# First block's value projection computed token by dimension in a two-layer kernel on one Trainium2 core

## The reference, cut to what matters

```
u = rmsnorm(x, g_mix_pre)
proj = u @ w_in                                  # (256, 2048) @ (2048, 10240)
qa, ka, va, qb, kb, vb, gla, glb = split(proj)   # 12 + 12 + 12 heads A, 4 + 4 + 4 heads B of 128, two gates of 2048
ya = dilated_mixture_attention(qa, ka, va) @ w_branch_a    # sum over keys: probs (q, k) @ v (k, 128)
yb = stick_breaking_attention(qb, kb, vb) @ w_branch_b     # likewise w (q, k) @ v (k, 128)
```

## Time and profile before

| what | value |
|---|---|
| median of 3 runs | 2671.86 us (2671.49 to 2672.24) |
| span of the profiled execution | 2672.7 us (first to last instruction; the page gives no other time of it) |
| PE busy | 2642.9 us, 99% of the span, 22834 matmuls |
| DVE busy | 1804.4 us, 68% |
| ACT busy | 1274.7 us, 48% |
| DMA | 496.71 MB, mean 186 GB/s |
| mean granted TensorE clock | 0.995 |

### The profile page before, as it was taken

The page is one execution under the profiler, slowest core; times in us unless marked ns, Lnnn a source line. Parts: engine busy times, 40 slices in busy tenths (PEclk is TensorE's granted clock), DMA queues, the critical chain, the costliest instruction groups (busy, mean ns, idle before and its releaser), DMA issues.

```text
span 2672.7 us, 57540 instructions
## 1 busy us (share of the span) xinstructions
PE 2642.9 (99%) x22834; PEld 2628.9 (98%) x22834; DVE 1804.4 (68%) x2269; ACT 1274.7 (48%) x1548; POOL 249.9 (9%) x206
## 2 busy tenths in 40 slices
PE   9999999999999999999999999999999999999998
PEld 9999999999999999999999999999999999999998
DVE  5455555747888888864467999867576777775444
ACT  5334455345344444444455556554455555554442
POOL 1000000030000000001101665400100000000000
PEclk9999999999999999999999999999999999999999
DMA  7665556574555655556656555556656666666664
GB/s 256 193 199 175 150 161 182 169 213 148 173 195 196 196 194 189 196 191 203 192 168 200 174 163 157 155 183 200 194 183 195 196 194 193 191 190 197 195 191 141
DMA packets 137806, 496.71 MB, mean 186 GB/s; under 512 B 15425, under 2 KB 15425, under 8 KB 137537
## 3 DMA queue, kind: packets, MB, share of 16 engines
q1 hardware_dynamic: 137520, 494.20, 59.7%
q10 hardware_dynamic: 144, 0.52, 0.1%
HBM read 492.57 MB, written 2.10 MB: 185 GB/s over the span
## 4 chain that ended last, share of the span: by engine, by line
PE 89%; DVE 6%; DVEq 2%; ACT 1%; DMA 1%; issue 1%; ACTq 0%; SPq 0%
PE bank L432 86%; DVE w_lo L982 2%; PE ps_a L432 1%; PE ps_o L432 1%; PE ps_n L432 1%; DVE act_lo L1021 1%; PE ps_t L432 0%; DMA hT<-in_xT 0%; ACT w_hi L676 0%; DMA w_raw<-in_w_in 0%; ACT act_hi L742 0%; DVE hT L1046 0%; DVE pr L1309 0%; DVE rstd L1005 0%; DVEq L1299 0%
## 5 line engine op out<-in xcount | busy, mean ns | idle before, releaser
L982 DVE TENSOR_TENSOR w_lo<-w_raw,w_hi 128x1024 fp32r<-128x1024 f32 x928 | 1134.1, 1234 | 720.8 <-ACT w_hi L676 719.2
L676 ACT ACTIVATE w_hi<-w_raw 128x1024 fp32r<-128x1024 f32 x928 | 977.0, 1056 | 1185.9 <-PE bank L432 1045.3
L432 PE MATMUL bank<-act_hi,w_hi 128*128 128x256 f32 x5408 | 1275.3, 279 | 3.0 <-DVE gate_y L1350 2.5
L432 PE MATMUL bank<-act_lo,w_hi 128*128 128x256 f32 x5408 | 1264.9, 277 | 0.0
L432 PEld LDWEIGHTS bank<-act_hi,w_hi 128*128 128x128 f32 x5408 | 1014.9, 188 | 4.1 <-issue 2.7
L432 PEld LDWEIGHTS bank<-act_lo,w_hi 128*128 128x128 f32 x5408 | 1015.7, 188 | 0.7
L432 PE MATMUL bank<-act_hi,w_lo 128*128 128x256 f32 x5408 | 726.9, 277 | 2.7 <-DVE w_lo L982 2.7
L432 PEld LDWEIGHTS bank<-act_hi,w_lo 128*128 128x128 f32 x5408 | 666.6, 188 | 3.1 <-DVE w_lo L982 3.1
L432 PE MATMUL bank<-f_lo,w_hi 128*128 128x256 f32 x1408 | 327.9, 276 | 0.0
L432 PE MATMUL bank<-f_hi,w_hi 128*128 128x256 f32 x1408 | 327.9, 276 | 0.0
L432 PEld LDWEIGHTS bank<-f_lo,w_hi 128*128 128x128 f32 x1408 | 264.3, 188 | 0.0
(11 more groups left out here) (227 smaller groups left out, 1790.3 us busy)
## 6 DMA issues: line engine op xcount, KB each, us to landing
w_raw<-in_w_up SPq DMA_DIRECT2D x352, 512.0 KB, 4.2
w_raw<-in_w_in SPq DMA_DIRECT2D x252, 512.0 KB, 4.2
w_raw<-in_w_down SPq DMA_DIRECT2D x176, 512.0 KB, 4.2
w_raw<-in_w_out SPq DMA_DIRECT2D x64, 512.0 KB, 4.4
w_raw<-in_w_ple_gate SPq DMA_DIRECT2D x32, 512.0 KB, 4.5
w_raw<-in_w_branch_attn SPq DMA_DIRECT2D x16, 512.0 KB, 3.9
w_raw<-in_w_branch_a SPq DMA_DIRECT2D x8, 512.0 KB, 4.1
w_raw<-in_w_branch_b SPq DMA_DIRECT2D x8, 512.0 KB, 3.5
```

The lines of the kernel that those rows point to most:

```text
L432: return pe.matmul(o, l, r, start=start, stop=stop, skip_group_check=True)
L676: act.activation(w_hi[:, k, 0:n, :], w_raw[:, k, 0:n, :], ACT.Copy).then_inc(hi_ready, 1)
L982: dve.tensor_tensor(w_lo[:, k, 0:n, :], w_raw[:, k, 0:n, :], w_hi[:, k, 0:n, :].bitcast(F32), ALU.subtract).then_inc(lo_ready, 1)
```

## The change

A new attribute `by_token` of a stage lists slots that are projected the other way round: a 128x128 tile of the activation (dimensions by tokens) is the stationary operand, and the 256 columns of the weight move. The result has tokens on the partitions and 256 output dimensions along the free side. The number of matmuls of a piece stays 24, and their size stays 128x128 by 256. `st_in` now ends after ka (6 bodies: 2 written out, 4 in the loop); a new stage `st_v` projects va (3 bodies: 1 written out, 2 in the loop), all of its slots by token; in `st_mix` slots 4 and 5 (vb) are by token.

With tokens on the partitions the norm's factor is one number for each partition. PE turns `rstd` once: after piece 15 of `st_in` two fp32 matmuls of one moving column each write the factors of tokens 0 to 127 and 128 to 255 into columns 256 and 257 of `ps_n`, and DVE copies them into `rstd_at` before its first piece of `st_v`. The eviction of a by-token slot is two multiplications of 128x256 by a scalar for each partition. `turn_values`, the 8 copies of ACT and all waits on `v_kept` are gone; two waits move to `pt_kept` and to the eviction count of DVE.

```diff
@@ buffers and semaphores
+        rstd_at = sb("rstd_at", [P, 2])
-        sb("before_stages", [P, 8])
+        sb("before_stages", [P, 6])
-        v_turned, v_kept = sem("v_turned"), sem("v_kept")
+        rstd_ready, rstd_turned = sem("rstd_ready"), sem("rstd_turned")
+        v_turned = sem("v_turned")
@@ stages
-        st_in = Stage("in", pair("w_in"), QB // 4, act_x, main_x(SPLIT["mix"]), "dve")
+        st_in = Stage("in", pair("w_in"), VA // 4, act_x, main_x(SPLIT["mix"]), "dve")
+        st_v = Stage("v", [cols("w_in", 16, 0, 2 * G, VA * P), cols("w_in", 16, 0, 2 * G, (VA + 2) * P)],
+                     HEADS_A // 4, act_x, None, "dve")
+        st_v.by_token, st_mix.by_token = (0, 1), tuple(range((VB - QB) // 2, (GATE_A - QB) // 2))
@@ PE, stream
+                        if s in st.by_token:
+                            for t in range(n):
+                                x = j * PIECE_KT + t
+                                for c in range(2):
+                                    o = ps[:, c * GROUP:(c + 1) * GROUP]
+                                    mm(o, xh[:, x, c * P:(c + 1) * P], w_hi[:, k, t, :], j == 0 and t == 0 and c == 0, False)
+                                    mm(o, xl[:, x, c * P:(c + 1) * P], w_hi[:, k, t, :], False, False)
+                            pe.wait_ge(lo_ready, q + 1)
+                            for t in range(n):
+                                x = j * PIECE_KT + t
+                                for c in range(2):
+                                    last = mm(ps[:, c * GROUP:(c + 1) * GROUP], xh[:, x, c * P:(c + 1) * P], w_lo[:, k, t, :],
+                                              False, j == st.pieces[s] - 1 and t == n - 1)
+                            last.then_inc(piece_used, 1)
+                            ...
+                            continue
@@ PE, beside the pieces
-            def turn_values(n):
-                ...
+            def turn_rstd(piece):
+                if piece == 15:
+                    pe.wait_ge(rstd_ready, 1)
+                    mm(ps_n[:, TOK:TOK + 1], rstd[:, 0:P], ident[:, 0:1], True, True)
+                    mm(ps_n[:, TOK + 1:TOK + 2], rstd[:, P:], ident[:, 0:1], False, True).then_inc(rstd_turned, 1)
-                if n in (4, 5, 6):
-                    turn_values(2 * n - 8)
-                    turn_values(2 * n - 7)
-                    if u == 0:
-                        pe.wait_ge(v_kept, 6)
-                if n == at_stick(0) - 1:
-                    pe.wait_ge(pt_kept, 8)
-                    turn_values(6)
-                    turn_values(7)
                     if h == 0:
                         pe.wait_ge(o_kept, 8)
+                        pe.wait_ge(evacuated["dve"], st_mix.evac0 + (GATE_A - QB) // 2)
                     if h == 0:
-                        pe.wait_ge(v_kept, 8)
+                        pe.wait_ge(pt_kept, 8)
-            stream(st_in, sums_beside(0))
+            sum_0 = sums_beside(0)
+            stream(st_in, lambda piece: (sum_0(piece), turn_rstd(piece)))
+            stream(st_v)
@@ ACT, mixer_1
-                for p in which(lambda p: LEAD + 4 + p // 2 if p < 6 else at_stick(0) + LEAD - 1, 8, n):
-                    tile = (VA + 2 * p) if p < HEADS_A // 2 else VB + 2 * p - HEADS_A
-                    act.wait_ge(v_turned, p + 1)
-                    act.activation(proj1[:, tile:tile + 2, :], ps_t[p % 2][:, :].rearrange("p (c t) -> p c t", c=2),
-                                   ACT.Copy).then_inc(v_kept, 1)
+            stream(st_v)
@@ DVE
             def root(n):
                 dve.wait_ge(std_ready, n + 1)
-                dve.reciprocal(rstd[:, :], rstd[:, :])
+                last = dve.reciprocal(rstd[:, :], rstd[:, :])
+                if n == 0:
+                    last.then_inc(rstd_ready, 1)
                 dve.drain()
@@ DVE, scaled_to
+                    if s in st.by_token:
+                        for c in range(2):
+                            last = dve.tensor_scalar(
+                                dst[:, bass.ds(t, 2), c * P:(c + 1) * P],
+                                bank_of(st, i, s)[:, c * GROUP:(c + 1) * GROUP].rearrange("p (k d) -> p k d", k=2),
+                                rstd_at[:, c:c + 1], None, ALU.mult)
+                        last.then_inc(evacuated["dve"], 1)
+                        return
@@ DVE, the stages
             last = stream(st_in, scaled_to(st_in, proj1), beside_in, ahead=1)
+            dve.wait_ge(rstd_turned, 1)
+            dve.tensor_copy(rstd_at[:, :], ps_n[:, TOK:TOK + 2])
+            dve.drain()
+            last = stream(st_v, scaled_to(st_v, proj1, VA // 2), None, last)
```

More of the change, by code:

```diff
@@ L102, in __init__ @@
         self.crossed, self.spare, self.late, self.hi_first = (), None, {}, None
+        self.by_token = ()
         self.written_out = 1
@@ L324, in build @@
         st_down2 = Stage("down2", quad("w_down_2", FT), 2, f_x, lambda j: (f_ready, 22 + 2 * j + 2), "dve")
-        stages = [st_in, st_mix, st_rest, st_branch, st_out, st_up, st_down, st_ple, st_gate,
+        stages = [st_in, st_v, st_mix, st_rest, st_branch, st_out, st_up, st_down, st_ple, st_gate,
                   st_in2, st_in2b, st_glu, st_in2c, st_branch2, st_out2, st_up2, st_down2]
@@ L476, in body @@
                         pe.wait_ge(hi_ready, q + 1)
+                        if s in st.by_token:
[12 more added lines that the diff above has]
+                            last.then_inc(piece_used, 1)
+                            if isinstance(i, int) and beside:
+                                beside(i * st.ppb + at)
+                            continue
                         for t in range(n):
@@ L1249, in mixer_2 @@
                 if n == at_head(0) - 1:
-                    dve.wait_ge(v_turned, 9)
+                    dve.wait_ge(v_turned, 1)
                     dve.tensor_copy(vtok, ps_t[0][:, 0:TOK].rearrange("p (k c) -> p k c", k=2)).then_inc(pad_ready, 1)
```

## The result

The changed kernel takes 2699.73 us (median of 4 runs, 2698.05 to 2700.55), the kernel before 2671.68 us (the three runs above and a fourth): a ratio of 1.0105, 95% interval [1.0092, 1.0118]. It is 28 us slower, where 3 us less were forecast and 2673.2 us was the upper end.

The account below looks back on a forecast made before the run. PE, busy 99% of the span, was taken as the bound: -3.63 us (transposes) + 0 (swapped operands) + 0.56 (turning rstd) = -3.07 us, so 2671.86 becomes 2668.8 us; range 2664.6 to 2673.2 us, a tenth left out each side.

Parts of the forecast that it names:

- the last sentence of the sum: Whole kernel outside the edit: it starts 3 us earlier and is otherwise the same, no cost.
- A: Rival, 768 by-token matmuls: weights move slower, 113.3 + d ns; gain gone at d = 4.0 ns; chance 0.13 (d above 2).
- B: Rival, by-token matmuls: weights move faster, at 106.7 ns, giving 2663.7 us, 0.31% faster; chance 0.10.
- C: Rival, half-clock stretches behind PE's waits: one lost or won, 2666.0 or 2671.6 us; chance 0.10, evenly both ways.
- D: Rival, removed transposes: they only filled time PE would have waited anyway, no gain, 2672.4 us; chance 0.05.
- the unknown costs: New stage st_v: unspecified costs counted, with the upper part of A, in the 0.08 chance of being above 2677.2 us.
- The swapped operands: 768 matmuls of st_v and st_mix: still 113.3 ns each, difference 0; ends 5.1 us saved or 6.1 us lost.
- The transposes: PE in st_mix: removing four bursts of 8 and the delays behind them saves 3.63 us, between 3.16 and 3.80.
- Turning `rstd`: PE behind piece 15 of st_in: four added fp32 instructions and the next piece's delay cost 0.56 us, bounds 0 to 1.10.
- Evictions, waits, code: DVE's paired multiplications, moved waits and the new stage's loop: cost 0; evictions 3.2 us in all without cover.
- The sum: -3.63 + 0 + 0.56 = -3.07 us, taken from the runs' median 2671.86 us, the profiled span being 0.8 us above it.

Follow-up runs that it names:

- e1: The changed kernel without the 24-byte filler `before_stages`, so the stages' buffers are back at 132736; 2671.75 us, 0.9996 of the kernel before.
- e2: The kernel before with 32 bytes more filler in front of the stages' buffers, nothing else changed; 2700.73 us, ratio 1.0104.
- e5: e1 with by-token matmuls in the old operand order (weight stationary), values left unturned, for timing alone; 2667.29 us, 0.9981 of the kernel before.
- e6: The changed kernel with act_hi, act_lo and the stages' buffers moved to odd multiples of 64 bytes, w_hi and w_lo to even ones; 2707.71 us (one run).
- e8: e1 with w_hi and w_lo in each other's place (w_hi at 98752, w_lo at 82240); 2714.6 us (one run).
- e10: e1 with w_lo moved down by 128 bytes, so w_hi and w_lo both lie 64 bytes above a multiple of 256; 2745.32 us (one run).
- e11: e1 with w_hi and w_lo both placed 192 bytes above a multiple of 256 (82112 and 98496); 2736.63 us (one run).
- e13: e1 with by-token remainders in a buffer of their own and the turning of rstd moved to right before st_v; 2671.64 us, 0.9993 of the kernel before.

## Why the prediction was wrong, point by point

- **The failed step** is the last sentence of the sum, that the rest of the kernel "is otherwise the same". It was costed at nothing without a look at what moves in memory. The diff changes two sizes, `rstd_at` in and `before_stages` from 8 to 6 columns; the prediction's working mentions neither. They move the region by 32 bytes, and 202 pieces of 24 matmuls lose 5.7 ns each, 27.4 us. e1 and e2 show it from both sides: the shift alone makes the loss, its undoing alone takes it back. No rival had this mechanism: A and B were about the swapped operands, C about the clock, D about the transposes, and the unknown costs about the new stage.
- **The swapped operands** were costed at 0, with ends of -5.1 and +6.1 us. They cost 2.50 us in `st_v`, 4.4 ns a matmul, which is rival A in mechanism. Its 4.0 ns at which the gain is gone were meant for all 768 matmuls; here 576 of them carry 4.4 ns, 2.50 of the 3.07 us. The argument, same shapes, types and buffers, left out the buffers' places. Without the shift of the region (e1, 2671.75 us) the time would have lain inside the stated range, but by this cost and not as forecast: that would have been luck. e5 isolates it. The lower end of 106.7 ns was not reached. The trace of before bears that figure out by its stretch at clock 0.50: from 676.59 to 681.50 us the starts lie 213.3 ns apart, 1.2 columns a ns, which the prediction writes as 1.2 GHz; half of that distance is 106.7 ns, an estimate for clock 1.00. The shortest distance found at clock 1.00 is 113 ns, before and after alike. In `vb`'s 8 pieces it costs nothing (22.78 us before, 22.77 after); all of them stand among the attention's fp32 matmuls, and were slow before.
- **The transposes**: 3.63 us forecast; `st_mix` got 4.11 us shorter here and 3.69 us in e1. The bursts and the delays of the pieces behind them went as read: pieces 4 to 7 take 10.88 us for 13.75, and the fourth burst gives 0.87 where 0.76 was forecast. The other 0.4 us are small differences in other pieces.
- **Turning `rstd`**: 0.56 us forecast, 0.36 + 0.17 = 0.53 measured (56.66 to 57.02, and 2.89 us for the next piece). The four loads start at 56.54, 56.66, 56.77 and 56.88 us and the next one at 56.99, 109 to 113 ns apart, 0.44 us in all. The 0.36 us is less than these 0.44 because it is counted from the first of the four matmuls, which starts 0.11 us behind its load; the four starts and the next lie 25, 112, 112 and 111 ns apart.
- **Evictions, waits, code**: cost 0, right. 478 ns each lies within 350 to 540; PE has no wait before 600 us that it did not have.
- **The clock**: one drop of 2.7 us fewer in the profiled execution, the size of rival C (2.8). It hides part of the loss in the spans and not in the medians. The sum laid the span of 2672.7 us beside the runs' times and found it 0.8 us high; a time is 1.8 us more than its span, so that execution took some 2674.5 us, above all four runs. And the 0.75 us between the first three runs, which the prediction held against rival C, was a small sample: later batches of 12 to 15 runs of the same kernel range over 4.3 to 6.0 us.

What stays open is what decides between the two pitches where both occur. Shown is: at the same places whole stages run at 113.3 and others, of the same matmuls, at 117.8 ns (e6, e8); the pitch changed at bursts of fp32 work, and in both directions: in `st_in` of e8 pieces 9 to 15 run at 113.3 ns and, from the four instructions that turn `rstd` on, all at 117.8, in e6 it is the other way round. It also changed with no such burst, where the order of the operands changes (in front of `st_v` in e10, behind it in e11). At the places of the kernel before, a piece that starts at 117.8 behind an fp32 burst is back at 113.3 within two pieces. With the weight moving, 113.3 was held in one kernel of eleven. That the two streams, the moving operand and the next load, fall in or out of step in PE's reads is an explanation that fits, and it was not shown. Nor was a place found that suits both orders of operands in one kernel; no version that computes the whole block beats the kernel before by more than the interval; the best of them is e13 (0.9993 [0.9983, 1.0003]).

## What to carry to other kernels

Lay the buffers' start addresses of both kernels side by side before costing an edit that adds or resizes one: a filler is counted in placed bytes, not in its own size (here 8 and 24 bytes took 32 each). In this kernel, bound by matmuls with a fresh stationary tile each, 32 bytes were worth 5% of every matmul that reads a moved buffer (113.3 to 119.0 ns in `f` and `x2`), more than most edits of the code; count matmuls in equal windows of stages that the edit does not touch. Turning a projection round to spare transposes then pays only if the new pairing of operands keeps its pitch: here the pairing took back 2.5 of the 3.7 us won, and the turning of the scale 0.5.

## What was not expected of the hardware

In these runs PE's pitch with 256 moving fp32r columns and a new 128x128 load each went with how the two operands' addresses lie to each other. With the weight stationary and the distances as in the table (mod 256 bytes, `w_hi` / `w_lo` matmuls) it is 113.3 ns at 64/192, 119 ns at 96/224 and 128/0, and either of 113.3 and 117.8 ns at 192/64, 64/64 and 192/192. A matmul's own distance does not decide alone: the `w_hi` matmuls of e10 have the addresses that they have in e1, and run at 117.8 in place of 113.3 once `w_lo` has moved. The same instructions on all engines (e2 at 2700.73 us and the kernel before at 2671.62 in the same batch) differ by 29 us by their places alone. What in PE or in the memory makes the difference, no run shows.
